# Corner transposes on VectorE, an earlier first GEMM tile and later weight splits in a hybrid GDN and sliding-window layer

## The reference, cut to what matters

```python
h = rms_norm(x, norm_w)
z = h @ w_in                      # all branches in one projection
# branch A: gated delta rule, 8 heads, dk = dv = 128
qkv = silu(causal_depthwise_conv(cat(qa, ka, va), conv_w))     # 4 taps
n_mat = where(strict, -(k*beta) @ k.T * decay, 0)
t_mat = (I - n_mat)^-1            # by repeated squaring
v_new = t_mat @ (v*beta) - (t_mat @ (k*beta*exp(g))) @ state
o = (q*exp(g)) @ state + (q @ k.T * decay) @ v_new
state = state*exp(g_last) + (k*exp(g_last - g)).T @ v_new
# branch B: 16 query heads, 2 key heads, window of 2 chunks of 64
logits = q @ k.T / 8 + bias
p = exp(logits - m);  probs = p / (sum(p) + exp(sink - m))
o = probs @ v
# merge
m = sigmoid(gA) * (oa @ w_o_a) + sigmoid(gB) * (ob @ w_o_b)
y = rms_norm(x + m @ w_out, final_norm_w)
```

## Time and profile before

| | us |
|---|---|
| median of 3 runs (lowest to highest) | 2635.09 (2634.76 to 2636.34) |
| the profiled execution | 2636.74 |
| its span in the trace | 2634.9 |
| PE busy | 2594.6 (98% of the span) |
| DVE busy | 1340.2 (51%) |
| ACT busy | 894.6 (34%) |
| POOL busy | 404.8 (15%) |

### The profile page before, as it was taken

One profiled execution on the slowest core, in us unless ns is written; L12 is line 12 of the kernel. 1 busy time (PEld: TensorE's weight loads), 2 busy tenths in 40 slices (PEclk: granted clock), 3 DMA queues, 4 the chain that ended last, 5 costly groups with the idle time before them and its releaser, 6 DMA issues.

```text
span 2634.9 us, 50095 instructions
## 1 busy us (share of the span) xinstructions
PE 2594.6 (98%) x20276; PEld 2129.6 (81%) x20276; DVE 1340.2 (51%) x3401; ACT 894.6 (34%) x2886; POOL 404.8 (15%) x238
## 2 busy tenths in 40 slices
PE   7999999999999999999999999999999999999998
PEld 5777777888888888888888888888888888888887
DVE  6577777323266666612325666651223666665022
ACT  4454445332234344321114344432112333434001
POOL 3443334343210011000001011000000011010000
PEclk9999999999999999999999999999999999999999
DMA  7555455687653333355553433335546433333554
GB/s 246 191 205 199 164 185 198 244 282 288 239 182 129 131 135 135 135 192 209 183 215 142 141 131 137 130 125 208 208 176 230 141 119 135 130 131 129 204 211 175
DMA packets 96085, 467.06 MB, mean 177 GB/s; under 512 B 13808, under 2 KB 34544, under 8 KB 48880
## 3 DMA queue, kind: packets, MB, share of 16 engines
q1 hardware_dynamic: 65664, 427.85, 45.1%
q10 hardware_dynamic: 30192, 36.02, 4.6%
HBM read 361.00 MB, written 102.83 MB: 176 GB/s over the span
## 4 chain that ended last, share of the span: by engine, by line
PE 90%; DVE 5%; DMA 1%; POOL 1%; ACT 1%; issue 1%; ACTq 0%; SPq 0%; POOLq 0%; DVEq 0%
PE bank L1321 24%; PE bank L1323 22%; PE bank L1322 22%; PE last_banks L1444 3%; PE last_banks L1432 2%; PE bank L1510 1%; PE bank L1495 1%; PE bank L1424 1%; PE bank L1487 1%; PE bank L1555 1%; PE last_banks L1564 1%; PE bank L1545 1%; PE bank L1540 1%; PE last_banks L1561 1%; PE bank L1502 1%; DMA w_raw<-in_w_tiles 1%
## 5 line engine op out<-in xcount | busy, mean ns | idle before, releaser
L1321 PE MATMUL bank<-hT_hi,w_sl 128*128 128x512 f32 x2112 | 889.6, 421 | 0.0
L1323 PE MATMUL bank<-hT_hi,w_sl 128*128 128x512 f32 x2112 | 826.9, 392 | 0.0
L1322 PE MATMUL bank<-hT_lo,w_sl 128*128 128x512 f32 x2112 | 825.6, 391 | 0.0
L1323 PEld LDWEIGHTS bank<-hT_hi,w_sl 128*128 128x128 f32 x2112 | 396.4, 188 | 86.9
L1321 PEld LDWEIGHTS bank<-hT_hi,w_sl 128*128 128x128 f32 x2112 | 397.6, 188 | 76.7 <-issue 0.9
L1322 PEld LDWEIGHTS bank<-hT_lo,w_sl 128*128 128x128 f32 x2112 | 398.6, 189 | 58.9 <-issue 0.7
L441 POOL TENSOR_TENSOR w_sl<-w_raw,w_sl 128x1024 fp32r<-128x1024 f32 x90 | 218.2, 2428 | 344.4 <-ACT w_sl L525 335.1
L1001 DVE SCALAR_TENSOR_TENSOR area<-zraw,stc,area 128x512 f32<-128x512 f32 x288 | 216.3, 751 | 3.3
L1164 DVE SCALAR_TENSOR_TENSOR s_cur<-s_cur,scs,last_banks 128x128 f32<-128x128 f32 x112 | 38.9, 347 | 189.7 <-PE last_banks L1561 189.7
L460 POOL TENSOR_TENSOR area<-sums_row,sums_at 128x512 f32<-128x512 f32 x32 | 37.1, 1160 | 635.8 <-DVE nmx L1117 594.6
L639 ACT ACTIVATE area<-area 128x512 f32<-128x512 f32 x96 | 60.4, 629 | 215.0 <-DVE area L1001 215.0
(11 more groups left out here) (242 smaller groups left out, 4345.2 us busy)
## 6 DMA issues: line engine op xcount, KB each, us to landing
w_sl<-saved_w SPq DMA_DIRECT2D x270, 1024.0 KB, 4.8
saved_w<-w_sl SPq DMA_DIRECT2D x90, 1024.0 KB, 4.9
w_raw<-in_w_tiles SPq DMA_DIRECT2D x90, 512.0 KB, 5.9
sums_row<-sum_rows ACTq DMA_DIRECT2D x32, 256.0 KB, 6.4
area<-in_x ACTq DMA_DIRECT2D x4, 2048.0 KB, 9.8
area<-in_x ACTq DMA_DIRECT2D x14, 512.0 KB, 7.4
out_y<-area ACTq DMA_DIRECT2D x3, 2048.0 KB, 7.2
bias_sb<-in_bias ACTq DMA_DIRECT2D x32, 128.0 KB, 2.7
```

Of the source, the lines that this page charges most:

```text
L1321: pe.matmul(dst, a_hi, b_hi, start=first, stop=False)
L1322: pe.matmul(dst, a_hi, b_lo, start=False, stop=False)
L1323: return pe.matmul(dst, a_lo, b_hi, start=False, stop=last)
```

## The change

In words:

- PE no longer transposes `tt`. DVE transposes four 32x32 blocks of each tile's corner into `od` itself (`turned_corner`, 4 instructions of 32 partitions by 4 tiles by 32), behind the output split. ACT's copy of the corner is gone.
- PE runs 8 steps ahead of the first logits (7 before) and 7 behind them (8 before), so that the next head's first weight tile is finished ahead of the logits.
- On ACT the first `fill` item (the constants' DMAs, the copy of that tile out of PSUM and a high part) moves ahead of the scaling of the values.
- On DVE the first `fill` item (with line 997, which waits for the constants' DMAs and for ACT's copy) moves ahead of the first logits, the second (line 1001) ahead of the quotient, and none stands between the quotient and level 1.
- `ssk` is computed by ACT in place of DVE.
- On POOL ten splits stand ahead of the first `rk` (eleven before). In each head of block 0 three splits stand ahead of the decays and wait for `prob_ready[0]`, one stands behind the decays and two behind `rqo`.

```diff
@@ POOL
 def head(h, n1, last):
     power(rk[:, :], ssk[:, :], NT, ssk_ready, n1, rk_ready)
-    low(2)
+    pool.wait_ge(prob_ready[0], n1)
+    low(3)
     if not last:
         pool.wait_ge(nmx_ready[1], n1)
         decays(h + 1, n1 + 1)
-    low(2)
+    low(1)
     power(rqo[...], qo[...], 2 * NT, qo_ready, n1, rqo_ready)
     low(2)
...
     if b == 0:
-        low(SLOTS)
+        low(SLOTS - 1)
...
-    low(GATE_TILES - FILL_GATES - SLOTS - 1)
+    low(GATE_TILES - FILL_GATES - SLOTS)
@@ ACT
     squares(ssq[:, 1, :], bch(3), ssq_ready[1], 1, junk_k)
+    act.wait_ge(ssq_ready[1], n1)
+    act.activation(ssk[:, :], ssq[:, 1, :], ACT.Copy, bias=4 * EPS).then_inc(ssk_ready, 1)
...
     ins.then_inc(pt0_ready, 1)
-    act.wait_ge(ft_done, n1)
-    act.activation(od[CH:P], bch(5)[CH:P, :, 0:CH], ACT.Copy).then_inc(merge_act, 1)
+    fill(1)
     act.wait_ge(tr_done[2], n1)
     scaled(vr, bch(4), kn, vr_ready)
-    fill(1)
@@ DVE
-    dve.wait_ge(ssq_ready[1], n1)
-    dve.tensor_scalar(ssk[:, :], ssq[:, 1, :], 4 * EPS, None, ALU.add).then_inc(ssk_ready, 1)
...
+    def turned_corner():
+        for a in BLOCKS[0:2]:
+            for c in BLOCKS[2:4]:
+                ins = dve.transpose(od[c, :, a], tt[a, :, c])
+        ins.then_inc(od_ready, 1)
...
+    dve.wait_ge(f_ready, n1)
+    turned_corner()
+    fill(1)
     logits(0)
     first_powers()
     attention()
     fill(1)
     quotient(0)
-    fill(1)
     level(1)
@@ PE
     transposes(2, vv)
-    fill(7)
+    fill(8)
...
-    pe.wait_ge(f_ready, n1)
-    for t in range(NT):
-        ins = pe.transpose(bch(5)[:, t, :], tt[:, t, :], ident)
-    ins.then_inc(ft_done, 1)
     logits_padded()
-    fill(8)
+    fill(7)
```

More of the change, by code:

```diff
@@ L103, in merges, with merge_copies @@
     return (n1 - 1) * 3 + step
+def merge_copies(n1, step):
+    return (n1 - 1) * 2 + step
 class Chain:
@@ L325, in build_program @@
         f_ready = sem("f_ready")
-        ft_done = sem("ft_done")
+        od_ready = sem("od_ready")
         pt0_ready = sem("pt0_ready")
@@ L722, in head @@
                 squares(ssq[:, 0, :], bch(2), ssq_ready[0], 0, junk_q)
-                act.wait_ge(ssq_ready[1], n1)
                 act.wait_ge(ksc_ready, n1)
@@ L1449, in inner_in @@
                     pe.wait_ge(merge_dve, merges(n1, 1))
-                    pe.wait_ge(merge_act, merges(n1, 1))
+                    pe.wait_ge(dec_ready, n1)
                     for t in range(NT):
@@ L1456, in inner_out @@
                 def inner_out():
-                    pe.wait_ge(merge_act, merges(n1, 2))
+                    pe.wait_ge(merge_act, merge_copies(n1, 1))
                     pe.wait_ge(attn_ready, n1)
@@ L1467, in merge_in @@
                     pe.wait_ge(diag_ready, n1)
+                    pe.wait_ge(od_ready, n1)
                     pe.wait_ge(merge_dve, merges(n1, 2))
@@ L1475, in merge_out @@
                 def merge_out():
-                    pe.wait_ge(merge_act, merges(n1, 3))
+                    pe.wait_ge(merge_act, merge_copies(n1, 2))
                     pe.wait_ge(merge_dve, merges(n1, 3))
```

## The result

The changed kernel takes 2666.68 us (median of 4 runs, 2663.75 to 2668.01), the kernel before 2635.59 beside it. The ratio is 1.0115 (95%: 1.0101 to 1.0128): slower by 31 us, where the forecast was 17. The sign held, and the time lies 1.3 us inside the upper end of the range; the size did not hold, and the mechanism only in part. The profiled execution is the fastest of the four, 2.9 us under their median.

The account below looks back on a forecast made before the run. PE, busy 98% of the span, was taken to bound the kernel. Blocks 1 to 3 gain 10.3 us and block 0 loses 26.4, together +16.1, so 2652 us; own range 2640 to 2661, stated range 2630 to 2668.

Parts of the forecast that it names:

- the cover fails: Blocks 1 to 3: late bias delays the quotient, 24 heads each lose 0.5 us; 2674 us, chance 0.08 shared with head end.
- X: Block 0: split moved from last behind `rqo` to first behind the quotient; PE's 17th step of the head starts 2.6 us later.
- the third split: Block 0: POOL's split two tiles behind X; forecast had its late raw load delay `yt` by 0.5 us.
- the forecast's sum of 26.4: Block 0's total loss in us: head 1 +0.8, six heads at 3.9 each, head 8 +2.2.
- Y: Block 0: split moved from ahead of `rqo` to behind it, ending at 286.5, so X's raw load goes out at 286.9.
- The forecast's exceptions for heads 1 and 8: Block 0: head 1 has no late load, +0.8 us; head 8 has no DMA ahead of its logits, +2.2 us.
- the head end that shows: Block 0: splits behind `rqo` hold `fo`, the head end loses 1.3 us; 2661 us, chance 0.08 shared with failing cover.
- `fo`'s hold: Block 0: splits after `rqo` hold `fo` and a tap; counted as covered because PE waits for `kd` anyway.
- 3.9 us a head: Block 0, heads 2 to 7: 2.6 at X's step, 0.5 at level 2, 0.5 at `yt`, 0.3 for landing spread.
- Faster: Rival: X and Y early enough, block 0's stalls vanish and all 32 heads gain; 2604.5 us, chance 0.13 including milder form.
- its milder form: Rival: block 0 stays as it is, only blocks 1 to 3 gain; 2625 us, nearly all of the 0.13.
- The stall is only moved: Rival, block 0: line 1041's stall moves to `fo` behind `rqo`; 2661 us, chance 0.08 shared with failing cover.

Follow-up runs that it names:

- Experiment 6: The kernel before with the corner transposed by DVE alone, no PE transposes or ACT copy, `ssk` still on DVE: 2624.53 us, ratio 0.9955.
- 3: The changed kernel with Y split ahead of `rqo` (two splits behind the decays, one behind `rqo`): 2631.01 us, ratio 0.9975.
- 5: The changed kernel with Y ahead of `rqo` and the first tile's eviction, constants and first step back at their old places: 2622.58 us, ratio 0.9946.
- experiment 11: The changed kernel with twelve unused PE transposes in block 0 where PE waited for the first quotient: 2671.92 us, ratio 1.0136.
- experiment 10: The changed kernel with the last pair of splits also waiting for the scaling of o, so it no longer holds `fo`: 2668.59 us, ratio 1.0126.
- 7: The kernel before with only the change's list of POOL splits: 2657.12 us, ratio 1.0085.
- 8: The changed kernel with split pairs behind the first quotient, the decays and `rqo`, so X and Y are at their old places: 2648.92 us, ratio 1.0047.
- 4: The changed kernel with X ahead of the wait for the quotient and Y ahead of `rqo`: 2657.11 us, ratio 1.0074.
- 9: The changed kernel, its list of splits kept, with the first tile's eviction, constants and first step at their old places: 2651.27 us, ratio 1.0054.
- experiment 1: The changed kernel with POOL's old list of splits and no wait for the quotient: 2657.17 us, ratio 1.0074.

## Why the prediction was right, and where its size was off

**Blocks 1 to 3.** Forecast -10.3, measured -10.4 in the profiled executions. Experiment 6 shows that the corner alone gives it (-11.1). The rival that the cover fails there is refuted: PE waits for the quotient twice in these blocks, 0.7 us in all, and the heads are the same with either order (experiments 3 and 5).

**Block 0 up to the second merge.** The chain of the forecast against the fifth head (us; the measured times less 16.66):

| step | forecast | measured |
|---|---|---|
| raw load of X goes out | 286.9 | 286.8 |
| ACT's high part of X | 292.7 | 292.6 |
| `rk` ends | 296.0 | 296.0 |
| triangular matrix ready | 297.7 | 297.7 |
| first logits | 298.0 | 297.9 |
| constants there | 301.9 | 301.6 |
| probabilities' transposes | 307.4 | 307.1 |
| step of tile X | 309.9 to 310.0 | 309.5 |
| merge with `yt` | 317.4 | 318.0 |

Up to X's step every place was right within 0.5 us. At the merge the head was 4.2 us later than before, where the forecast had 3.6: the clock behind the quotient is in that, and `yt` waited for PE, not for the raw load.

**The step that failed** is where the sum ended: it closed a head at `yt` and added 0.3. Behind it the third split holds the diagonal copies, PE waits 0.85, and the next merge starts at 320.3, 5.3 later than before. Eight heads lost 38.6 us, 4.8 each, where the forecast's sum of 26.4 is 3.3 each; 1.25 was gained ahead of them. The forecast misses 11 us of this, of which the rows name 4.9: the 2.8 of three such waits, and the 2.1 that `fo`'s hold costs at the end of the eighth head. The low clock goes with more of it (below), and the rest has no one owner. By the medians (31.1 slower, with 10.4 gained in blocks 1 to 3) block 0 loses 41 us and the forecast misses 15. I had looked for POOL's hold on DVE at X and Y and not at the third split, although its move was in the same list. The forecast's exceptions for heads 1 and 8 can't be compared one by one, since a distance between two logits holds the end of one head and the late load of the next; but from the eighth head's logits to block 1's first the time rose by 5.75 us (291.13 to 296.88), as in the others, so head 8 was no exception (forecast: 2.2).

**Luck in the range.** The forecast's own range was 2640 to 2661, with block 0 at most 36 us slower. Block 0 was 37.3 us slower in the profiled execution, and the median is 5.7 above 2661. The stated range reached to 2668 for rivals of which one, the head end that shows, came in part and the other did not. That 2666.68 lies within it is thus partly luck.

**The clock.** Heads 1, 3 and 7, 56.4 to 56.6 us, have a granted clock of 0.94, 1.00 and 0.94 in the 30 us from their logits, the four of 58.5 to 59.3 have 0.89. That looks like 2 us a head that no term held. But head 3 at full clock is no more than 0.3 us shorter than heads 1 and 7 at 0.94, and experiment 11 mended the first drop and won nothing. So the two go together, and the clock's own price is open.

**`fo`'s hold.** The forecast called it covered. In heads 1 to 7 it shows as PE's wait of 6.0 us (0.85 each). In the fifth head's timeline the transposes behind this wait end at 308.77, 1.5 us before ACT's late high part does (310.27), which the squares wait for anyway, so there the reading speaks for cover. At the end of the eighth head no late load covers it: PE waits 2.08 us, and this wait is gone in experiment 10. Experiment 10 moved the hold of the other heads without removing it and doesn't settle them.

**What was right in theory and incomplete.** The prediction laid block 0's loss on the list of splits. The list alone costs 20.8 us (7), and Y's place makes 35.7 of difference in the whole (3). X's late place, to which the forecast gave most of its 3.9 us a head (2.6 at the step of tile X), is not a loss that an earlier X takes back: with Y early and DVE's new order, every earlier place tried for X costs 18 to 26 us more (8, 4). In the fifth head the quotient alone was 1.4 us later than before, the step 2.2, and PE waited 0.58 there for the split. Further, DVE's logits behind the constants' transfer cost 8.4 to 33 us by the list they are combined with (5, 9, 1 against 6). It was in the forecast as a time (302.3) and not as a part that could be taken back.

**The rivals.** "Faster" needed X and Y early enough: with Y early and the old order it came, 2622.6 us, close to the 2625 of its milder form. "The stall is only moved" (2661) was nearest in size, and partly by its reason: Y, X and the third split each hold DVE somewhere new, and Y's hold shows at the end of the eighth head.

## What to carry to other kernels

In a list that two engines share through buffers, the place of an item fixes not only when it runs but when its buffer's next load goes out. Follow every item that a move shifts to the end of the loop, and not only those next to the critical wait. Here a copy that the busiest engine waits for stood behind an instruction that waits for a transfer. Exchanging two such instructions gave 11.8 us, as much as taking four transposes off PE in all 32 heads. When a part of a change gives what was forecast and the whole doesn't, time the parts. Here the corner alone was worth 11.8 us while its company cost 42.

## What the runs showed of the hardware

In the fifth head of block 0 the granted clock was 0.54 for 7.4 us behind a wait of 1.63 us on PE; behind the same wait it was 0.77 in two other heads and 1.00 in head 3. Filling the wait (experiment 11) kept it at 1.00 there, and in another stretch of the same head it then was 0.84. Twelve 128x128 transposes took 1.47 us on PE, 0.12 each, and four block transposes of 32x32 on four tiles 1.26 us together on DVE. The landing of a small transfer varied most: the bias (128 KB) has a median of 2.2 us in block 0 of the changed kernel, 3.3 in the kernel before and 4.1 in experiment 1, while the raw loads (512 KB) stay at 5.7, 5.9 and 5.8. Why was not tried.
